# A two-layer hybrid decoder trunk on one core: VectorE's order in attentions and norms, weight tiles waited for part by part, unweighted token rows

## What is computed

```python
# layer 0
z = rms_norm(h, g) @ w_in                       # split into b_gate, c_gate, u, q, k, v
h = h + concat(short_conv(b_gate, c_gate, u), sliding_window_attention(q, k, v)) @ w_out
h = h + swiglu(rms_norm(h, g), gate, up, down)  # width 2816
h = h + sigmoid(rms_norm(h, g) @ w_g) * (p[0] @ w_p)
# layer 1
h = h + moba_attention(rms_norm(h, g) @ w_qkv) @ w_o   # 256 tokens: one causal block
h = h + moe_swiglu(rms_norm(h, g), router, gate, up, down)  # top 2 of 8 experts, width 3584
h = h + sigmoid(rms_norm(h, g) @ w_g) * (p[1] @ w_p)
out = rms_norm(h, final_norm)
```

## Time and profile before

| | us |
|---|---|
| median of 3 runs (1461.81 to 1464.96) | 1462.02 |
| the profiled execution | 1463.82 |
| its span, first to last instruction | 1462.0 |

### The profile page before, as it was taken

The page is one execution under the profiler, slowest core; times in us unless marked ns, Lnnn a source line. Parts: engine busy times, 40 slices in busy tenths (PEclk is TensorE's granted clock), DMA queues, the critical chain, the costliest instruction groups (busy, mean ns, idle before and its releaser), DMA issues.

```text
span 1462.0 us, 20926 instructions
## 1 busy us (share of the span) xinstructions
PE 1433.2 (98%) x7521; PEld 1219.0 (83%) x7521; DVE 1156.6 (79%) x950; ACT 957.9 (66%) x847; POOL 84.6 (6%) x99
## 2 busy tenths in 40 slices
PE   9999999999999999999999999999999999999997
PEld 8978999988987788888888888888888888888775
DVE  5676555566656988888888988888888888888996
ACT  5445434356446777777777777777777777777774
POOL 2000000000001940000000000000000000002000
PEclk9999999999999999999999999999999999999999
DMA  9546855565433999999999999999999999999980
GB/s 323 209 157 241 278 173 184 191 230 171 164 128 104 349 401 394 397 394 380 378 395 380 370 387 369 383 384 378 387 371 392 380 367 393 372 356 395 394 319 29
DMA packets 208179, 455.07 MB, mean 311 GB/s; under 512 B 7497, under 2 KB 49493, under 8 KB 208142
## 3 DMA queue, kind: packets, MB, share of 16 engines
q1 hardware_dynamic: 201184, 429.94, 80.7%
q0 software_dynamic: 5184, 18.44, 3.4%
q10 hardware_dynamic: 1774, 6.17, 1.1%
HBM read 439.83 MB, written 14.70 MB: 311 GB/s over the span
## 4 chain that ended last, share of the span: by engine, by line
PE 88%; DVE 6%; ACT 3%; DMA 2%; issue 1%; SPq 0%; ACTq 0%; DVEq 0%
PE bank L909 48%; PE bank L1366 19%; PE bank L940 13%; PE bank L1162 4%; DVE w_lo L1429 2%; PE bank L1341 2%; ACT w_hi L562 1%; DMA raw<-in_o_exp_down 1%; DMA raw<-in_e_w_in 1%; ACT x_hi L590 0%; PE bank L1323 0%; ACT xn L578 0%; DVE x_lo L1463 0%; PE bank L1056 0%; DVE h L1785 0%
## 5 line engine op out<-in xcount | busy, mean ns | idle before, releaser
L1429 DVE TENSOR_TENSOR w_lo<-raw,w_hi 128x2048 fp32r<-128x2048 f32 x406 | 932.8, 2302 | 201.8 <-ACT w_hi L562 200.5
L562 ACT ACTIVATE w_hi<-raw 128x2048 fp32r<-128x2048 f32 x406 | 779.0, 1919 | 312.5 <-PE bank L909 162.4
L909 PE MATMUL bank<-w_lo,x_hi 128*128 128x512 f32 (+2 forms) x1032 | 400.6, 388 | 4.2 <-DVE w_lo L1429 3.9
L909 PE MATMUL bank<-w_hi,x_hi 128*128 128x512 f32 (+2 forms) x1032 | 394.2, 382 | 0.0
L909 PE MATMUL bank<-w_hi,x_lo 128*128 128x512 f32 (+2 forms) x1032 | 393.4, 381 | 0.0
L909 PEld LDWEIGHTS bank<-w_lo,x_hi 128*128 128x128 f32 x1032 | 194.3, 188 | 44.9 <-DVE w_lo L1429 7.2
L909 PEld LDWEIGHTS bank<-w_hi,x_hi 128*128 128x128 f32 x1032 | 194.1, 188 | 38.0
L909 PEld LDWEIGHTS bank<-w_hi,x_lo 128*128 128x128 f32 x1032 | 194.5, 188 | 34.8
L1366 PE MATMUL bank<-w_lo,m_hi 128*128 128x512 f32 x448 | 175.7, 392 | 0.3 <-DVE m_lo L1801 0.3
L1366 PE MATMUL bank<-w_hi,m_hi 128*128 128x512 f32 x448 | 174.6, 390 | 0.0
L1366 PE MATMUL bank<-w_hi,m_lo 128*128 128x512 f32 x448 | 174.6, 390 | 0.0
(11 more groups left out here) (249 smaller groups left out, 1122.7 us busy)
## 6 DMA issues: line engine op xcount, KB each, us to landing
raw<-in_o_exp_gate SPq DMA_DIRECT2D x112, 1024.0 KB, 7.3
raw<-in_o_exp_up SPq DMA_DIRECT2D x112, 1024.0 KB, 7.8
raw<-in_o_exp_down SPq DMA_DIRECT2D x112, 1024.0 KB, 7.4
raw<-in_o_w_qkv SPq DMA_DIRECT2D x12, 1024.0 KB, 5.2
raw<-in_e_ffn_gate SPq DMA_DIRECT2D x11, 1024.0 KB, 5.4
raw<-in_e_ffn_up SPq DMA_DIRECT2D x11, 1024.0 KB, 5.3
raw<-in_e_ffn_down SPq DMA_DIRECT2D x11, 1024.0 KB, 5.0
raw<-in_e_w_in SPq DMA_DIRECT2D x9, 1024.0 KB, 15.5
```

Of the source, the lines that this page charges most:

```text
L562: act.activation(w_hi[:, slot % SPLIT], raw[:, slot], ACT.Copy).then_inc(hi_made, 1)
L909: mm = pe.matmul(dst, stat_hl[a], mov_hl[b], start=start and i == 0, stop=stop and i == 2)
L1429: ve.tensor_tensor(w_lo[:, slot % SPLIT], raw[:, slot], w_hi[:, slot % SPLIT], ALU.subtract).then_inc(lo_made, 1)
```

## The change

TensorE waits for the first two q tiles by part: first all high by high products, behind `hi_made` and the chunk of `x_hi`, then weight low by x high behind `lo_made`, then weight high by x low behind the chunks of `x_lo`. Expert tiles are treated the same way: `gate_up` and `down` wait for the high part, and for the low part of the weight only before the products that read it; `down` waits for the high part of the hidden tile first and for its low part later. `PASSES` gets the order (1, 0), (0, 1), (0, 0). The scatter waits for y by halves.

VectorE divides one head ahead in the attention of layer 0, before the low part of the output and the maxima; in layer 1 the maxima of the next even head come before the other tile. In norms 1 and 3 the low part of the weight tile is made between the two halves of `x_lo`.

GpSimd no longer multiplies by the gain. The rows go to DRAM unweighted, and the gain is applied by chunk when a job's rows are evicted. The gain tile is loaded once, early, with the final norm's gain.

```diff
@@ route_rows (GpSimd)
-                pool.wait_ge(gain_loaded, 16)
-                pool.wait_ge(gather_ready, 2)
-                for t in range(TT):
-                    pool.tensor_tensor(xn[:, t], xn[:, t], gain[:, :], ALU.mult).then_inc(rows_weighted, 1)
-                pool.wait_ge(rows_weighted, TT)
-                load_gain(6)
+                pool.wait_ge(rows_scaled, TT)
...
-            load_gain(4)
+            load_gain(6)
@@ gathered (ScalarE; VectorE's is changed likewise, with scalar_tensor_tensor)
-                    act.activation(x_hi[:, 4 * half:4 * half + 4, 0:P], ...).then_inc(xg_hi_made, 1)
+                    for k in range(4 * half, 4 * half + 4):
+                        ins = act.activation(x_hi[:, k, 0:P], bank[4 + half][:, k % 4 * P:(k % 4 + 1) * P], ACT.Copy,
+                                             scale=gainT[:, k, 4:5])
+                    ins.then_inc(xg_hi_made, 1)
@@ TensorE
-        PASSES = ((0, 1), (1, 0), (0, 0))
+        PASSES = ((1, 0), (0, 1), (0, 0))
+            def wait_high(n):
+                pe.wait_ge(hi_made, n + 1)
@@ first two tiles
-                wait_tile(Q0_T + i)
...
+                wait_high(Q0_T + i)
+                for part, (s, x) in enumerate(((0, x_hi), (1, x_hi), (0, x_lo))):
+                    if part == 1:
+                        wait_tile(Q0_T + i)
...
@@ scatter
-                pe.wait_ge(y_made, 2 * j + 2)
+                    if t == 0:
+                        pe.wait_ge(y_made, 2 * j + (half + 1))
@@ gate_up
-                    wait_tile(at(k + i, j, b))
+                    wait_high(at(k + i, j, b))
+                    for kk in range(4):
+                        pe.matmul(dst, x_hi[:, c + kk, 0:P], hi[:, kk], start=(c, kk) == (0, 0), stop=False)
...
+                    for kk in range(4):
+                        pe.matmul(dst, x_lo[:, c + kk, 0:P], hi[:, kk], start=False, stop=False)
+                    wait_tile(at(k + i, j, b))
+                    for kk in range(4):
+                        mm = pe.matmul(dst, x_hi[:, c + kk, 0:P], lo[:, kk], start=False, stop=(c, kk) == (4, 3))
@@ down
-                pe.wait_ge(hidT_lo_made, hid)
+                pe.wait_ge(hidT_hi_made, hid)
                 for i in parts:
+                    wait_high(at(k + i, j, b))
+                    for half in range(2):
+                        product(half, 0, 0, first=start and i == 0)
+                    pe.wait_ge(hidT_lo_made, hid)
+                    if not (stop and i):
+                        for half in range(2):
+                            product(half, 1, 0)
+                        wait_tile(at(k + i, j, b))
+                        product(0, 0, 1)
+                        product(1, 0, 1).then_inc(tile_used, 1)
...
@@ attention (VectorE)
+                if layer == 0:
+                    probabilities(0)
+                    lead()
+                for hd in range(HEADS):
+                    if layer == 1:
+                        probabilities(hd)
+                        if hd % 2 and hd + 1 < HEADS:
+                            maxima(hd + 1)
                     extra(hd)
-                    if layer == 1 and hd % 2 and hd + 1 < HEADS:
-                        maxima(hd + 1)
+                    if layer == 0 and hd + 1 < HEADS:
+                        probabilities(hd + 1)
                     if hd:
                         output(hd - 1)
@@ norms 1 and 3 (VectorE)
-            lows(1)
+            lows(1, (0,))
             split(OUT0_T + 2 + SPLIT)
+            lows(1, (1,))
...
-            lows(3)
+            lows(3, (0,))
             split(PLE0_T + 3 + SPLIT)
+            lows(3, (1,))
```

More of the change, by code:

```diff
@@ L1084, in _ @@
             turn_x(0, 1)
+            pe.wait_ge(gainT_made, 1)
             for i in range(2):
-                wait_tile(Q0_T + i)
                 w = w_tile(Q0_T + i, HALF)
-                for j in range(4):
-                    if i == 0 and j == 0:
-                        pe.wait_ge(gainT_made, 1)
-                    if j == 2:
-                        pe.wait_ge(diag_copied, 2)
-                    for k in range(4):
-                        if j == 0:
-                            wait_chunks(0, 4 * i + k)
-                        three(bank[j][:, 0:SEQ], both(w, ALL, k, slice(j * P, (j + 1) * P)), both(XHL, ALL, 4 * i + k), (i, k) == (0, 0), (i, k) == (1, 3),
-                              tile_used if (j, k) == (3, 3) else None)
+                wait_high(Q0_T + i)
+                for part, (s, x) in enumerate(((0, x_hi), (1, x_hi), (0, x_lo))):
+                    if part == 1:
+                        wait_tile(Q0_T + i)
+                    for j in range(4):
+                        if j == 2:
+                            pe.wait_ge(diag_copied, 2)
+                        for k in range(4):
+                            if part == 0 and j == 0:
+                                pe.wait_ge(x_hi_made, 4 * i + k + 1)
+                            if part == 2 and j == 0:
+                                wait_chunks(0, 4 * i + k)
+                            mm = pe.matmul(bank[j][:, 0:SEQ], w[s][:, k, j * P:(j + 1) * P], x[:, 4 * i + k],
+                                           start=(i, part, k) == (0, 0, 0), stop=(i, part, k) == (1, 2, 3))
+                mm.then_inc(tile_used, 1)
             wait_tile(KV_T)
@@ L1362, in down @@
                     w = w_tile(MOE_T + k + i, D)
-                    for half in range(2):
-                        for kk in range(2):
-                            for q, (s, m) in enumerate(PASSES):
-                                mm = pe.matmul(bank[6 + half][:, :], hidT[s][:, 2 * i + kk, :],
-                                               w[m][:, kk, half * HALF:(half + 1) * HALF],
-                                               start=start and (i, kk, q) == (0, 0, 0),
-                                               stop=stop and (i, kk, q) == (1, 1, 2), skip_group_check=True)
-                        if half:
-                            mm.then_inc(tile_used, 1)
-                        elif stop and i:
-                            mm.then_inc(y_ready, 1)
+                    wait_high(at(k + i, j, b))
@@ new lines, in product @@
+                    def product(half, s, m, first=False, end=False):
+                        for kk in range(2):
+                            mm = pe.matmul(bank[6 + half][:, :], hidT[s][:, 2 * i + kk, :],
+                                           w[m][:, kk, half * HALF:(half + 1) * HALF],
+                                           start=first and kk == 0, stop=end and kk == 1, skip_group_check=True)
+                        return mm
+                    for half in range(2):
+                        product(half, 0, 0, first=start and i == 0)
@@ new lines, in down @@
+                    pe.wait_ge(hidT_lo_made, hid)
[5 more added lines that the diff above has]
+                        product(1, 0, 1).then_inc(tile_used, 1)
+                    else:
+                        wait_tile(at(k + i, j, b))
+                        for half in range(2):
+                            product(half, 1, 0)
+                            product(half, 0, 1, end=True).then_inc(tile_used if half else y_ready, 1)
@@ L1513, in attention, with probabilities @@
                     lead()
-                maxima(0)
-                maxima(1)
-                if layer == 0:
-                    lead()
-                for hd in range(HEADS):
+                def probabilities(hd):
                     a = first + hd
@@ L1769, in gathered @@
                     ve.wait_ge(xg_hi_made, 2 * j + (KC - 2 + half + 1))
-                    at = x_lo[:, 4 * half:4 * half + 4, 0:P]
-                    ve.tensor_tensor(at, bank[4 + half][:, :].rearrange("p (c t) -> p c t", c=4),
-                                     x_hi[:, 4 * half:4 * half + 4, 0:P], ALU.subtract).then_inc(xg_lo_made, 1)
+                    for k in range(4 * half, 4 * half + 4):
+                        ins = ve.scalar_tensor_tensor(out=x_lo[:, k, 0:P], in0=bank[4 + half][:, k % 4 * P:(k % 4 + 1) * P],
+                                                      scalar=gainT[:, k, 4:5], in1=x_hi[:, k, 0:P], op0=ALU.mult, op1=ALU.subtract)
+                    ins.then_inc(xg_lo_made, 1)
             def scattered():
```

16 lines of the change are left out of this document (8 added, 8 removed).

## The result

| | us |
|---|---|
| kernel before, median of 4 runs (1461.81 to 1464.96) | 1462.34 |
| changed kernel, median of 4 runs (1448.05 to 1449.39) | 1448.71 |
| predicted | 1451.0 (1446.0 to 1457.0) |
| ratio, with its 95% interval | 0.9903 (0.9886 to 0.9920) |
| the profiled execution of the changed kernel, and its span | 1448.05, 1446.3 |

The change is worth 13.6 us where 11.0 were forecast. The experiments ran on three chips, where the kernel before had medians from 1462.2 to 1463.5. A difference of about 1 us between two experiments is no larger than that, so where one matters it is also read from the two traces, part by part.

A forecast was written before the change was run, and what follows sets the result against it. TensorE was taken as the chain nearly everywhere, so each removed stall gains its length. Gains at single stalls, less 1.1 us lost in attention 0, sum to -11.0 from 1462.02: 1451.0 us, own range 1449 to 1453.5, wider range 1446 to 1457.

The forecast's parts named there:

- First tiles: First q tiles: high products start 1.10 us earlier and the low clock level ends earlier; gain 2.1, bounds 0.6 and 2.7.
- Attention 0: Layer 0 attention: two stalls go, but divisions lengthen the VectorE-ScalarE loop; its end 1.1 us later, bounds -4.6 and +2.8.
- The five turns: Layer 0 attention: VectorE's loop from maxima of head 2, five times 8.24 us plus 0.9, ending at 108.4 against 105.4 before.
- Norms and attention 1: Norms 1 and 3, second tile: gains 1.28 and 0.45 us; layer 1 attention, two stalls removed: gain 2.07.
- Start of the expert stage: Three tiles late for w_lo: tile 1 gains 0.9 us, the two beside GpSimd's multiplication 2.2; row writes move to about 496.5.
- the supply rival: Expert stage: row writes or a transfer bound take its gains, 1454.1; far end, job changes not covered, 1461.5; chance 0.12.
- The loop: Expert loop: about 8 more waits in each of 56 blocks cost 0, up to 1 us; job changes 0, bound 10.5.
- Scatter: End of the last job: the scatter, 0.85 us late behind the second half of y, starts earlier; gain 0.85.
- The order working as drawn (1): Layer 0 attention: the 8.24 us loop is absorbed, so 1.1 becomes -4.6: 1445.3; chance 0.13.
- The clock at both places (2): First tiles gain 0.6 instead of 2.1, and low clock after the stall at head 5 costs 1.7: 1454.2; chance 0.14.
- A price per wait (4): Middle of expert tiles: 448 added waits break the stream; 25 ns each takes the whole gain, 0.1 us gives 1496; chance 0.05.
- Late tiles that wait for the high part (5): Late tiles turn out to wait for w_hi, so high parts first moves nothing; 0.9 and 1.8 stay: 1453.7; chance 0.06.

The follow-up runs named there:

- the mixed order: Changed kernel with layer 0 attention dividing ahead only for head 0 (before the conv tile) and head 6 (before maxima of head 7): 1445.34 us.
- its two variants: Mixed order with head 6 divided behind output 4, plus either head 1 divided ahead (1445.08 us) or a shorter TensorE wait at the first output tile (1444.45).
- the whole-wait kernel: Changed kernel with TensorE again waiting for low parts before an expert tile's first product and before the first down product, rows still unweighted: 1464.56 us.
- the old-order run: Changed kernel with VectorE's old order of divisions in the attention of layer 0, nothing else undone: 1447.01 us.
- The best version: Changed kernel dividing ahead only heads 0 and 6 (6 behind output 4), with a shorter TensorE wait at the first output tile: 1444.4 us over eight runs.

## Why the prediction was right, and where its sum was off

The sum was 2.6 us short between the medians and 4.8 between the two profiles. Of the 4.8 the loop makes 2.6, attention 0 1.0, and most of the rest are tenths behind single stalls.

**First tiles: right in mechanism.** High products start at 14.77, where 14.74 was forecast; in twelve profiles with the new tiles they start between 14.2 and 15.5, since the transposes ahead of them vary, so a hit to 0.03 is luck. The low level ends with the second of them, at 15.3. The part shows 2.4 between the profiles and 1.8 between medians; in four of the twelve profiles the low level lasts on to 16.2 to 17.2, never to 19.4, so the forecast's 2.1 is the better case and not the mean. (Its upper bound should read 2.8, 1.10 and 1.7; and 1.95 and 2.3 make 4.25, not 4.35. Neither moves the sum.)

**Attention 0: right in mechanism; the size is luck.** The old stalls go, VectorE's loop is the limit, and it is 7.96 to 8.66 us from division to division (8.24, three times with 0.3 more, was forecast). One turn, of 7.96:

```profile
69.24 0.15 DVE L1543 TENSOR_TENSOR stat<-stat 128x2 f32<-128x2 f32 x1
...
77.20 0.15 DVE L1543 TENSOR_TENSOR stat<-stat 128x2 f32<-128x2 f32 x1
```

The forecast of +1.1 is for an old order with half clock behind its first stall and a new order without any. The profiles can be sorted by both. The same 381 matmuls, from 53.99 to 120.00 us in the kernel before, take (us):

| order of the divisions | no half clock | half clock |
|---|---|---|
| old | 64.55 (one profile) | 66.02 (the kernel before) |
| all one head ahead | 65.75 and 65.76 | 65.93 to 66.16 (five) |
| all ahead, shorter wait at the first output tile | | 67.26 (one) |
| the mixed order and its two variants | 62.21 to 63.25 (four) | |

For the case of the forecast the new order gains 0.3 where it was to cost 1.1: this part of the sum was 1.4 us too high. The five turns were reckoned at 42.1 from the maxima of head 2 to those of head 7 and took 41.5, the maxima of head 2 came 0.5 earlier than the walk had them, and the half clock of the old order cost 1.5 for 1.7. Against an old order without the half clock, as in its run, the new one costs 1.2 (1.4 to 1.6 with its own half clock). That this is so near to 1.1 comes of two errors that cancel: a delay put too long, and a half clock counted as sure.

The table also shows why the clock matters less in the new order. I had put over 2 us at the output of head 5. In the profile of the changed kernel there were 1.85 at the first output tile, half clock behind it, and 1.0 at head 5 (and 0.5 at head 1). In the two profiles where the clock stayed up, the stall at head 5 is as forecast. The rows are the changed kernel and the run with the old orders in norms and attention 1:

```profile
103.69 0.41 PE L1036 MATMUL bank<-probT,work 128*64 128x128 f32 x2 [0.85 <-DVE m_lo L1534]
```

```profile
104.01 0.40 PE L1036 MATMUL bank<-probT,work 128*64 128x128 f32 x2 [2.08 <-DVE m_lo L1534]
```

The half clock makes TensorE 1.4 to 1.6 us slower behind the output tile, and 1.2 of that would have been spent waiting at head 5 anyway. In the old order, where the loop is not the limit, it costs its full 1.5. With the stall at the output tile removed, 3.06 us stood at head 5 (2.90 by its row and the 0.16).

**Norms and attention 1: right**, to 0.15 us in each of the three parts of the table.

**Start of the expert stage: right in its gain, wrong in one step.** Tile 1 and the two behind the multiplication give 0.98 and 2.47 (0.9 and 2.2). The rows of GpSimd, VectorE and ScalarE:

```profile
494.92 2.72 POOL L511 DMA_INDIRECT xg_scratch<-xn,row_of  x1 [0.91 <-POOL row_of L499]
...
497.08 2.29 DVE L1453 TENSOR_TENSOR w_lo<-raw,w_hi 128x2048 fp32r<-128x2048 f32 x1 [0.43 <-ACT w_hi L556]
...
523.45 1.92 ACT L556 ACTIVATE w_hi<-raw 128x2048 fp32r<-128x2048 f32 x1 [0.83 <-DMA raw<-in_o_exp_up]
```

No low part is longer than 2.29 us. The row writes start 9 us earlier, counted from the first instruction, but TensorE is 7 to 10 us earlier there too, and the first write starts at the same place of its stream as before (behind matmul 3235, before 3239). The forecast's step that moves them ahead, to 496.5, failed: GpSimd's ranking took 31.8 us instead of 27.5, since more of its steps of 0.2 us fell beside a low part and took 2.1 to 2.4. Weight tiles are up to 0.83 us late for ScalarE behind the writes, without a stall of TensorE: the supply rival did not come, but writes that come ahead of the stream were not put to the test. The transfers run at 384 GB/s again, against the 358 of the Trainium skill (SBUF — State Buffer, A bandwidth-pool intuition that's wrong), and removed stalls did not come back as waits on them.

**The loop: the wrong term.** It stood at 0 and gave 2.58. The added waits cost nothing, as the run with 1120 more shows. The step that failed is the reading that there was nothing to win in the loop: I had read "200.00 busy of 200" as "no stall", and a matmul that starts 0.1 us late lies within its predecessor's modelled end. The kernel before, TensorE at a job change:

```profile
821.94 0.39 PE L1366 MATMUL bank<-w_hi,m_hi 128*128 128x512 f32 x1
822.22 0.49 PE L909 MATMUL bank<-w_lo,x_hi 128*128 128x512 f32 x1
822.55 0.40 PE L909 MATMUL bank<-w_hi,x_lo 128*128 128x512 f32 x1
822.79 0.39 PE L909 MATMUL bank<-w_hi,x_hi 128*128 128x512 f32 x1
```

The steps are 0.28 and 0.33 where 0.227 is the pace. This makes 0.16 a job change (0.17 to 0.21 around each of the seven in the laid-over traces), 1.3 us; 0.9 more went in such small steps between 507 and 574, and 0.4 in the first half of the last job. The part-wise waits take them all.

**The same 0.1 us sits behind every wait.** The step after a late start is 0.33 instead of 0.227 (0.22 instead of 0.12 for 256 columns), in the last job at all three tiles. I had counted 0.16 for the modelled end and not this: some 0.1 for each of ten stalls, which is why many gains of the table are 0.1 or so a stall over the forecast (last job 2.19 for 1.8, down tiles 0.60 for 0.48).

**Scatter: right** (0.91 for 0.85). The first placement starts at 1408.51, one step behind the last down matmul.

**The rivals.** The order working as drawn (1) is refuted by the old order being faster. The clock at both places (2) half came: never at the first tiles, but behind the new stall of attention 0 in five of seven profiles that have it, where it cost not 1.7 but 0.2 to 0.4. The supply (3) did not bind, and its far end, the uncovered job changes, is exactly what the whole-wait kernel has. A price per wait (4) did not show: with 1120 more waits the median is 0.1 us lower. Late tiles that wait for the high part (5): none.

## What to carry to other kernels

For two engines in a loop, look at which work fills a wait and which lengthens the chain: the same 0.95 us were free behind the maxima and cost 1.2 us in sum ahead of them, and only the first division and the one before the last maxima belonged ahead. A part-wise wait cost nothing here when met and covers lateness up to the length of the products ahead of it, so it can pay for another edit (here 11 us of evictions) that would be a loss by itself. When a forecast agrees, ask whether its terms do: lay every profile over the same matmuls and sort by what the clock did. Find stalls by steps between starts, not by idle time or busy share: what is under 0.16 us is in neither.

## What the runs showed of the hardware

The same stall does not always bring the low level of TensorE's clock. The 1.30 us at the first transposes of attention 0 were followed by half clock in the profile of before (60.4 to 63.8) and not in that of the old-order run (58.2 to 61.6); the 1.85 at the first output tile was in five of seven profiles; the last stall of attention 1 not in the kernel before, but in the run with the old orders. The stretch at the low level takes 1.3 to 1.6 us longer each time, of which 1.2 came back in the changed kernel's attention 0 as a shorter stall. It may be a part of why runs of one kernel differ (the kernel before: 1460.16 to 1466.62 over all its runs; that this is the clock was not shown run by run). The best version, with no stall over 0.62 us in the attention, spreads over 1.2 us in eight runs, the changed kernel over 2.3. Single profiles must not be subtracted without looking at the clock of each stretch.

VectorE's instructions of 2.29 us took 4.3 each beside GpSimd's two multiplications (8.60 for two), and kept 2.29 beside GpSimd's row writes. Taken one by one, they take turns: the first multiplication ends at 496.95, the low part begun beside it at 499.10, the second multiplication at 501.37, the next low part at 503.52, some 2.2 us apart each time. This agrees with what the Trainium skill says (SBUF — State Buffer, Who interferes with whom): a GpSimd instruction that reads SBUF and a VectorE one with two SBUF inputs exclude each other.
